# Pairs of heads in one attention stage, results as split columns, a new opening, and a recast difference attention

## The chip, the cores and the metric

The kernel runs on one core of a Trainium2 chip. The metric is the device time of one execution in microseconds (us); the figure for a kernel is the median of several runs. TensorE (PE) does matrix products and transposes (a transpose is a matmul against the identity). VectorE (DVE), ScalarE (ACT) and GpSimd (POOL) do elementwise work, SyncE (SP) issues most DMAs. The engines run their own instruction streams and meet at semaphores. On-chip data lies in SBUF with 128 partitions, products land in PSUM (8 banks).

## The reference

Two transformer blocks run one after the other, both on 256 tokens of width 1024 in float32. What the change touches:

```python
def first_block(x, mem, positions, ...):
    cos_ret, sin_ret = rope_tables(positions, RET_DK)
    cos_mla, sin_mla = rope_tables(positions, MLA_ROPE)
    mem_n = rms_norm(mem, mem_norm)
    for l in range(DEPTH):
        ng = norm_gains[l]
        x = x + 0.5 * rms_norm(swiglu(rms_norm(x, ng[0]), ffn_w_gu[l, 0], ffn_w_down[l, 0]), ng[1])
        h = rms_norm(x, ng[2])
        if l % 2 == 0: tok, qm = retention_mixer(h, ...)
        else:          tok, qm = mla_mixer(h, ...)          # 6 heads, keys 96 wide, values 128
        mem_out = memory_attention(qm, mem_n, mem_w_kv[l])  # 4 heads of 64
        x = x + rms_norm(jnp.concatenate([tok, mem_out], -1) @ w_o[l], ng[3])
        x = x + 0.5 * rms_norm(swiglu(rms_norm(x, ng[4]), ...), ng[5])

def _even_mixer(...):     # second block, layer 0: 256 latent and 256 context tokens
    pl, pc = (jnp.split(a @ w_in, EVEN_SPLITS, -1) for a in (xl, xc))
    hl, hc = _mlstm_bidir(...)                     # 4 heads
    ml = headnorm(h, ml_g) * sigmoid(o)
    lam = exp(sum(lp[0]*lp[1])) - exp(sum(lp[2]*lp[3])) + lam_init
    p = softmax(s)                                  # two maps of scores per head, 4 heads
    da = (p[:, :, 0] - lam * p[:, :, 1]) @ v        # rotated q and k (latent tokens)
    y = jnp.concatenate([ml, headnorm(da, da_g) * (1 - lam_init)], -1) @ w_out
```

The second block's odd layer has a window attention with 16 query heads over 4 key heads; both its layers end with a feed-forward over retrieved experts (PEER).

## The kernel before, in words

**Products.** Every float32 operand is split into a high part (rounded to fp32r) and a low part (the rest), and a product is three matmuls: high by low, low by high, high by high (L251 to L253). Activations lie as columns (feature on the partition) in a "pair" of high and low. Weights come through a ring of three 1 MB slots (tile `ring`, 128x2048), filled by SP in a fixed order (`stream_weights`). ACT makes the high half of a unit of 128x1024 (L223, `split_hi`) and DVE the low half (L230, `split_lo`; POOL does some), into three unit buffers (`units`). In most of the program PE is busy all the time, and DVE and ACT wait for buffers to come free.

**Stages.** `K.block()` is a stage: its engines' code is written out by hand, each engine runs its own list in order, and the end of a stage is a barrier for all of them. The program is a sequence of such stages:

- Opening: SP and ACT issue loads; `norm_to_pair` takes `mem` through root mean square norm, 16 transposes on PE and a split into a pair; `rotary_tables` makes sine and cosine; `spread_conditions` takes the SiLU of the condition vectors; then `norm_to_pair`-like code does the same for x at the entry of the first feed-forward (`feed_forward`, FT = 22 steps; SiLU on ACT, L1337 and two more on DVE per step).
- Layer 0 of the first block: projection (`project`), retention, then memory attention (`attend`), then `columns_to_pair` (PE transposes the mixer's output, ACT and DVE split it) and `quad` work (`multiply_quad`, part of the conditions' product), then the product with w_o.
- Layer 1: the same with latent attention (MLA): `attend` with 12 units, a stage for the memory's transposes, `attend` with 8 units, transposes and split.
- Second block, even layer: the mLSTM attention (`attend_mlstm`), whose stage also holds the projection of the difference attention's rows, and ends with a normalisation of heads on DVE; then `difference_attention`: lambda, rotations of q and k rows, transposes, 16 units of attention, `normalise_heads`, transposes and split into a pair.
- Odd layer: `window_attention`: projections of queries and of keys and values, then a stage for the rotations and for the doubled copies of keys, then transposes and attention.

**A unit of attention** is one head with 128 query rows. PE makes its scores (L1518), DVE their row maxima, ACT the exponentials with their sum, DVE divides, PE transposes the weights (L1526), ACT or DVE copies them out, PE multiplies with the values (L1535). Unit u+1's scores and unit u-1's values stand around the transposes of unit u in PE's list; the buffers are two deep. The difference attention has two maps per unit: DVE takes two maxima (L2050), a scale (L2052), reciprocals (L2063), two factors (L2064, L2065) and the difference (L2068, tile `weights`), and at the end copies the result (L2092, tile `da_out`).

## Time and profile before

| | us |
|---|---|
| median of 3 runs (lowest, highest) | 4476.64 (4474.61, 4479.72) |
| the profiled execution's own time | 4477.14 |
| its span | 4475.3 |
| PE busy | 4097.1 (92%) |
| DVE busy | 2988.9 (67%) |
| ACT busy | 2104.9 (47%) |
| POOL busy | 443.5 (10%) |
| mean granted clock of PE | 0.955 |

The profile is one execution. In a row of stretches "busy" is time in which the engine had an instruction at work, and the clock is the mean share of PE's full speed that was granted: 1.00 is 2.4 GHz and 0.50 is 1.2 GHz. The rest of a span in which PE was not busy is what this change works on; it is spread over the joints between stages.

### The profile page before, as it was taken

How to read it: one execution, taken by the hardware profiler on the slowest of the kernel's cores; microseconds unless marked ns; L12 is line 12 of the kernel's file. 1: busy time of each engine (PE TensorE's matmuls, PEld its weight loads, DVE VectorE, ACT ScalarE, POOL GpSimd, SP SyncE). 2: the span in 40 equal slices, each digit the busy share in tenths (PEclk: the TensorE clock that was granted, in tenths of full speed). 3: DMA queues.
4: the chain of work that ended last, by engine and by line, in shares of the span. 5: the costliest groups of instructions: out<-in, count | busy, mean ns of one | idle time of the engine just before them, and what ended most of it. 6: DMA issues, size and time to landing. Idle time of an engine off the chain costs nothing. (4 is left out here: it accounts for less than half of the span.)

```text
span 4475.3 us, 71173 instructions
## 1 busy us (share of the span) xinstructions
PE 4097.1 (92%) x25224; PEld 3600.8 (80%) x25224; DVE 2988.9 (67%) x5834; ACT 2104.9 (47%) x3223; POOL 443.5 (10%) x488
## 2 busy tenths in 40 slices
PE   6996999968989668999999989999999789999998
PEld 5995889848978558888888888888888578888887
DVE  4555555555546648877777798777776588777776
ACT  4442444434434325555555555555554455555554
POOL 0000000000011105400000162000001045000000
PEclk9997999978989879999999999999999999999999
DMA  5554655554521023255555523555554031555554
GB/s 193 185 197 173 227 199 194 205 202 152 185 109 56 25 89 112 85 188 192 192 187 189 201 86 130 190 188 193 191 211 148 36 138 57 188 190 194 188 189 168
DMA packets 105290, 718.20 MB, mean 160 GB/s; under 512 B 13856, under 2 KB 14464, under 8 KB 21280
## 3 DMA queue, kind: packets, MB, share of 16 engines
q1 hardware_dynamic: 94688, 661.45, 40.5%
q0 software_dynamic: 8880, 52.12, 3.0%
q8 instruction: 107, 1.75, 0.2%
q10 hardware_dynamic: 1552, 2.36, 0.1%
q14 instruction: 63, 0.52, 0.0%
HBM read 709.48 MB, written 6.39 MB: 160 GB/s over the span
## 5 line engine op out<-in xcount | busy, mean ns | idle before, releaser
L230 DVE TENSOR_TENSOR units<-ring,units 128x1024 fp32r<-128x1024 f32 x1128 | 1378.9, 1224 | 562.0 <-ACT units L223 534.3
L223 ACT ACTIVATE units<-ring 128x1024 fp32r<-128x1024 f32 x1206 | 1273.5, 1057 | 1006.7 <-PE ps L253 966.0
L3176 PE MATMUL ps<-wide,units 128*128 128x512 f32 x2904 | 717.5, 389 | 3.3 <-PEq L3062 3.3
L3176 PEld LDWEIGHTS ps<-wide,units 128*128 128x128 f32 x2904 | 544.7, 188 | 117.0 <-issue 3.8
L251 PE MATMUL ps<-units,weighted 128*128 128x512 f32 x1536 | 602.9, 393 | 4.3 <-DVE units L230 4.3
L252 PE MATMUL ps<-units,weighted 128*128 128x512 f32 x1536 | 602.1, 392 | 0.0
L253 PE MATMUL ps<-units,weighted 128*128 128x512 f32 x1536 | 597.5, 389 | 0.0
L3226 ACT ACTIVATE low_halves<-ps 128x256 f32<-128x256 f32 x363 | 139.4, 384 | 623.2 <-PE ps L3178 623.2
L3178 PEld LDWEIGHTS ps<-wide,units 128*128 128x128 f32 x2904 | 396.2, 190 | 28.3
L3178 PE MATMUL ps<-wide,units 128*128 128x256 f32 x2904 | 404.9, 282 | 0.0
L251 PE MATMUL ps<-h_pair,units 128*128 128x256 f32 x1408 | 395.6, 281 | 0.0
L253 PE MATMUL ps<-h_pair,units 128*128 128x256 f32 x1408 | 394.3, 280 | 0.0
L252 PE MATMUL ps<-h_pair,units 128*128 128x256 f32 x1408 | 393.9, 280 | 0.0
L3260 DVE TENSOR_TENSOR gelued<-low_halves,ps 128x256 f32<-128x256 f32 x363 | 153.0, 421 | 315.1 <-ACT low_halves L3226 315.1
L253 PEld LDWEIGHTS ps<-units,weighted 128*128 128x128 f32 x1536 | 288.6, 188 | 62.9
L251 PEld LDWEIGHTS ps<-units,weighted 128*128 128x128 f32 x1536 | 289.9, 189 | 57.3 <-DVE units L230 6.9
L252 PEld LDWEIGHTS ps<-units,weighted 128*128 128x128 f32 x1536 | 289.9, 189 | 46.1
L1337 DVE TENSOR_TENSOR weighted_whole<-gelued,G 128x256 f32<-128x256 f32 x363 | 154.5, 426 | 220.7 <-ACT gelued L3230 215.1
L251 PEld LDWEIGHTS ps<-h_pair,units 128*128 128x128 f32 x1408 | 265.5, 189 | 3.6
L252 PEld LDWEIGHTS ps<-h_pair,units 128*128 128x128 f32 x1408 | 265.0, 188 | 3.8
L253 PEld LDWEIGHTS ps<-h_pair,units 128*128 128x128 f32 x1408 | 265.7, 189 | 0.0
L3095 PE MATMUL ps<-hits 128*128 128x128 f32 x1536 | 231.7, 304 | 9.2 <-POOL hits L3072 9.2
(503 smaller groups left out, 6739.7 us busy)
## 6 DMA issues: line engine op xcount, KB each, us to landing
ring<-in_stream SPq DMA_DIRECT2D x603, 1024.0 KB, 4.8
quad_ring<-in_mod_w POOLq DMA_DIRECT2D x12, 4096.0 KB, 13.9
front<-residuals_dram SPq DMA_DIRECT2D x5, 1024.0 KB, 7.1
gain_rows<-in_norm_gains SPq DMA_DIRECT2D x6, 512.0 KB, 5.0
peer_keys<-in_keys SPq DMA_DIRECT2D x3, 1024.0 KB, 5.1
ml_mask<-in_ml_mask SPq DMA_DIRECT2D x1, 2048.0 KB, 7.7
residuals_dram<-residual SPq DMA_DIRECT2D x2, 1024.0 KB, 7.3
front<-mod_rows_dram SPq DMA_DIRECT2D x4, 512.0 KB, 8.0
```

The costliest lines, as they stand in the source:

```text
L223: act.activation(K.parts(n)[0], K.raw(n), ACT.Copy).then_inc(K.sig("hi_made").sem, 1)
L230: dve.tensor_tensor(lo, K.raw(n), hi.bitcast(FP32), ALU.subtract).then_inc(K.sig("unit_split").sem, 1)
L251: pe.matmul(out, w[0], x[0], start=start, stop=False)
L252: pe.matmul(out, w[0], x[1], start=False, stop=False)
L253: return pe.matmul(out, w[1], x[0], start=False, stop=stop)
L1337: dve.tensor_tensor(whole, a, b, ALU.mult).then_inc(made.sem, 1)
L3095: last = pe.matmul(bank(n)[:, m * KEYS:(m + 1) * KEYS], hits[:, n % BUFFERS, 1, m, :], hits[:, n % BUFFERS, 0, m, :], start=True, stop=True)
L3176: pe.matmul(both, hi[:, k, :], pair[:, :, k, :], start=(k == 0), stop=False)
L3178: last = pe.matmul(both[:, 0, :], lo[:, k, :], pair[:, 0, k, :], start=False, stop=(k == KD - 1))
L3226: act.activation(lows[:, e % 2, :], K.ps[:, 4 + e % 2, SEQ:2 * SEQ], ACT.Copy).then_inc(lows_copied.sem, 1)
L3260: dve.tensor_tensor(gelued[:, e % 2, :], lows[:, e % 2, :], K.ps[:, 4 + e % 2, 0:SEQ], ALU.add)\
```

## The change

**Opening.** x is loaded first, by SP, and then the first three weight slots; `mem`, the positions and the tables' constants come after them. The stages for `mem` and the rotary tables are gone: a class `Opening` puts their work into the feed-forward's steps 18 to 20 (the squares and sines on ACT, angles, tables and the scaling on DVE), and `MemoryHead` puts the 16 transposes and the split of `mem` into chunks 1 and 2 of layer 0's projection. x goes to its pair by the same eight transposed groups as other entries do.

**First block's attentions.** `attend_columns` takes two heads at once (`Two`), three deep: two score products, one DVE maximum over both, two exponentials, a reciprocal and two scalings in place, four transposes, one ACT copy of 128x512, four products with the values as the stationary operand, so that the result comes out as columns; ACT writes its high part and DVE its low part into the pair that the w_o product reads. In layer 0 it holds the memory's 4 paired units; a stage for the 6 remaining columns (with the quad work) follows. In layer 1 one stage holds 6 latent and 4 memory units, and no transposes or split follow.

**Even layer of the second block.** In `attend_mlstm`, ACT takes the squares' sums per unit inside the loop, lambda is computed there, and behind the loop DVE rotates q and k rows, multiplies the gates with the gains and normalises with 16 products. `turned_heads` transposes the mLSTM's columns and q and k in 12 groups of four. The difference attention is again three deep, with one maximum over both maps, a joint factor and one product; its norm (one Square per unit on ACT) ends in the same stage, where each head is transposed and split as soon as it is scaled.

**Window attention.** DVE rotates the query rows under the projection of keys and values (`aside`), and ACT takes half of the key copies.

The diff, cut to its core:

```diff
+class Opening:
...
+    def sync(self, sp):
+        K, ins, loaded = self.K, self.K.ins, self.loaded
+        sp.dma_start(K.x[:, :, :], ins["x"].rearrange("(t p) d -> p t d", p=P)).then_inc(self.x_loaded.sem, 16)
+        stream_weights(K, sp, 0)
+        sp.dma_start(self.pos[:, :], ins["positions"]).then_inc(loaded.sem, 16)
...
+    def scalar(self, act, E):
...
+        act.wait_ge(*self.x_loaded.at(16))
+        for t in range(MT):
+            last = act.activation(E.xs[:, t, :], E.src[:, t, :], ACT.Square, accum_out=E.sums[1][:, t:t + 1])
+        last.then_inc(squared.sem, 1)
+        rstd(K, None, act, E.sums[1], D, squared, mean_done, root_done)
+        split_ahead(K, act, split_hi, K.taken)
...
+    def scalar_step(self, act, f, E):
+        if f == FT - 4:
+            act.wait_ge(*self.loaded.at(96))
+            for t in range(MT):
+                last = act.activation(E.xs[:, t, :], self.mem[:, t, :], ACT.Square, accum_out=self.ss[:, t:t + 1])
...
+    def vector_step(self, dve, f):
...
+        if f == FT - 2:
+            dve.wait_ge(*self.sined.at(1))
+            self.tables(dve)
+            dve.wait_ge(*self.root_done.at(1))
+            self.K.orders["dve"](dve, dve.reciprocal(self.ss, self.ss))
+            for t in range(MT):
+                dve.tensor_scalar(self.mem[:, t, :], self.mem[:, t, :], self.ss[:, t:t + 1], None, ALU.mult)\
...
+class MemoryHead(NormHead):
...
+    def late_tensor(self, pe, c):
+        K = self.K
+        if c == 1:
+            pe.wait_ge(*K.sig("mem_scaled").at(MT))
+        if c in (2, 3):
...
+                    last = pe.transpose(self.bank(k)[:, t * P:(t + 1) * P], self.mem[:, t, k * P:(k + 1) * P], K.ident[:, :])
...
+def attend_columns(K, units, pair):
...
+                for step in range(count + 3):
+                    i = step
+                    if i < count:
+                        if i >= 2:
+                            pe.wait_ge(*weighed.at(i - 1))
+                        for j in range(2):
+                            last = pe.matmul(scores(i)[:, j, :], units[i].q[j], units[i].k[j], start=True, stop=True)
+                        last.then_inc(scored.sem, 1)
+                    i = step - 2
+                    if 0 <= i < count:
+                        pe.wait_ge(*shared.at(i + 1))
+                        if i >= 2:
+                            pe.wait_ge(*copied.at(i - 1))
+                        for j in range(2):
+                            for b in range(MT):
+                                last = pe.transpose(K.ps[:, 4 + i % 2, (j * MT + b) * P:(j * MT + b + 1) * P],
+                                                    exps[:, i % DEEP, j, b * P:(b + 1) * P], K.ident[:, :])
+                        last.then_inc(turned.sem, 1)
+                    i = step - 3
+                    if i >= 0:
+                        pe.wait_ge(*copied.at(i + 1))
+                        if i >= 2:
+                            pe.wait_ge(*taken.at(i - 1))
+                        for j in range(2):
+                            for b in range(MT):
+                                last = pe.matmul(result(i, j), units[i].v[j][b], flipped[:, i % 2, j, b * P:(b + 1) * P],
+                                                 start=(b == 0), stop=(b == MT - 1))
+                        last.then_inc(made.sem, 1)
             @block.vector
             def _(dve):
+                for step in range(count + 4):
...
+                        dve.wait_ge(*scored.at(i + 1))
+                        dve.tensor_reduce(bias[:, i, :], scores(i), AX, ALU.max, negate=True).then_inc(raised.sem, 1)
+                    i = step - 1
+                    if 0 <= i < count:
+                        dve.wait_ge(*weighed.at(i + 1))
+                        order(dve, dve.reciprocal(sums[:, i, :], sums[:, i, :]))
+                        for j in range(2):
+                            row = exps[:, i % DEEP, j, :]
+                            last = dve.tensor_scalar(row, row, sums[:, i, j:j + 1], None, ALU.mult)
+                        last.then_inc(shared.sem, 1)
+                    i = step - 4
+                    if i >= 0:
+                        dve.wait_ge(*rounded.at(i + 1))
+                        dve.tensor_tensor(part(1, i), whole(i), part(0, i).bitcast(FP32), ALU.subtract).then_inc(taken.sem, 1)
...
+                        act.wait_ge(*raised.at(i + 1))
+                        if i >= DEEP:
+                            act.wait_ge(*turned.at(i - DEEP + 1))
+                        for j in range(2):
+                            last = act.activation(exps[:, i % DEEP, j, :], scores(i)[:, j, :], ACT.Exp, bias=bias[:, i, j:j + 1],
+                                                  accum_out=sums[:, i, j:j + 1])
+                        last.then_inc(weighed.sem, 1)
...
+                        act.wait_ge(*made.at(i + 1))
+                        act.activation(part(0, i), whole(i), ACT.Copy).then_inc(rounded.sem, 1)
...
                 dve.wait_ge(*out_taken.at(n_units))
-                for t in range(TILES):
-                    var = K.stat[:, 32 + 7 * t:32 + 7 * t + ML_HEADS]
-                    sq = seen[:, t % 2, :, :].rearrange("p m (h d) -> p (m h) d", d=DV)[:, 0:ML_HEADS, :]
-                    head_stats(K, dve, None, h[:, t, :, :], sq, None, var, ML_HEADS, False)
...
+                dve.wait_ge(*head_squared.at(n_units))
+                dve.tensor_scalar(root, root, 1.0 / DV, EPS, ALU.mult, ALU.add).then_inc(var_done.sem, 1)
+                tmp = seen[:, :, :, :].rearrange("p i m n -> p (i m) n")
+                dve.wait_ge(*rows_taken.at(4))
+                rotate(K, dve, rows[:, MT:TILES, 0:512].rearrange("p t (h d) -> p t h d", d=64), 32, sin, cos, tmp)
+                order(dve, dve.tensor_tensor(gate, gate, row[:, :].unsqueeze(1).broadcast_to([P, TILES, width]), ALU.mult))
+                dve.wait_ge(*rows_taken.at(8))
+                rotate(K, dve, rows[:, MT:TILES, 512:1024].rearrange("p t (h d) -> p t h d", d=64), 32, sin, cos, tmp)
+                dve.wait_ge(*root_done.at(1))
+                order(dve, dve.reciprocal(root, root))
+                    for n in range(ML_HEADS):
+                        d = slice(n * DV, (n + 1) * DV)
+                        last = dve.scalar_tensor_tensor(mix[:, t, d], h[:, t, n, :], root[:, t, n:n + 1], gate[:, t, d],
+                                                        ALU.mult, ALU.mult)
+                order(dve, last)
...
+def turned_heads(K, rows, mix, q, k):
...
+    sources = [[mix[:, t, c * P:(c + 1) * P] for t in range(TILES)] for c in range(4)]
+    for at in (0, 512):
+        sources += [[rows[:, t, at + h * P:at + (h + 1) * P] for t in range(TILES)] for h in range(4)]
...
+                        dve.wait_ge(*scored.at(i + 1))
+                        dve.tensor_reduce(bias[:, i, :], scores(i), AX, ALU.max, negate=True).then_inc(raised.sem, 1)
+                    i = step - 1
+                    if 0 <= i < len(work):
+                        dve.wait_ge(*exped.at(i + 1))
+                        order(dve, dve.reciprocal(share[:, i, :], sums[:, i, 1:2]))
+                        order(dve, dve.scalar_tensor_tensor(share[:, i, :], sums[:, i, 0:1], lam, share[:, i, :], ALU.mult, ALU.mult))
+                        n = keys(i)
+                        dve.scalar_tensor_tensor(exps[:, i % DEEP, 0, 0:n], exps[:, i % DEEP, 1, 0:n], share[:, i, :],
+                                                 exps[:, i % DEEP, 0, 0:n], ALU.mult, ALU.add).then_inc(shared.sem, 1)
...
+                        dve.tensor_scalar(out[:, h, t, :], result(i), sums[:, i, 0:1], None, ALU.mult).then_inc(taken.sem, 1)
...
+                        last = dve.scalar_tensor_tensor(out[:, h, t, :], out[:, h, t, :], square[:, 4 * h + t, :],
+                                                        row[:, h * DV:(h + 1) * DV], ALU.mult, ALU.mult)
+                    last.then_inc(weighed.sem, 1)
...
+                    last = dve.tensor_tensor(pair[:, 1, 4 + h, :], K.ps[:, h, :], pair[:, 0, 4 + h, :].bitcast(FP32), ALU.subtract)
...
-        project(K, pair, KD, TILES, 2 * kv_width, kv)
+        def rotate_queries(dve):
+            rotate(K, dve, qrows[:, :, :].rearrange("p t (h d) -> p t h d", d=WA_DH), 32, sin, cos, tmp)
+        project(K, pair, KD, TILES, 2 * kv_width, kv, aside=rotate_queries)
...
+                        last = act.activation(k2[:, t, :, n, :], heads_of(t), ACT.Copy)
```

The first place is the start of the program on ACT. `x`, `cols`, `ident` are input tiles, `normed` is the normalised x, `h_pair` its pair, `c_silued` the condition. Before:

```order
L1899 ACT_TABLE_LOAD
L1899 ACTIVATE c_silued<-cols 128x16
L1896 UNCONDITIONAL_BRANCH
L1288 UNCONDITIONAL_BRANCH
L353 ACTIVATE normed,stat<-x 128x1024 x2
L302 ACT_TABLE_LOAD
L302 ACTIVATE stat<-stat 128x2
L358 ACTIVATE h_pair<-ps,cols 128x256 x8
L223 ACTIVATE units<-ring 128x1024
```

After:

```order
L1438 DMA ident<-in_ident 128x128
L1439 DMA cols<-in_cols 128x171
L1443 ACT_TABLE_LOAD
L1443 ACTIVATE normed,stat<-x 128x1024 x2
L302 ACT_TABLE_LOAD
L302 ACTIVATE stat<-stat 128x2
L223 ACTIVATE units<-ring 128x1024 x2
L1450 ACTIVATE h_pair<-ps,cols 128x256 x8
L1451 ACT_TABLE_LOAD
L1451 ACTIVATE c_silued<-cols 128x16
L223 ACTIVATE units<-ring 128x1024
```

ACT no longer does a norm of `mem` ahead of that of x (lines 1391 to 1377 above), and x's squares (both halves now) come ahead of its first weight splits (L223).

The second place is PE at the latent attention of layer 1: `mla_q`, `mla_k` queries and keys, `mla_kv` the values, `turned_weights` the transposed softmax weights. Before:

```order
L1518 MATMUL ps<-mla_k,mla_q 128x256 x2
L1526 MATMUL ps<-ident,weights 128x128 x2
L1518 MATMUL ps<-mla_k,mla_q 128x256
L1526 MATMUL ps<-ident,weights 128x128 x2
L1535 MATMUL ps<-mla_kv,turned_weights 128x128 x2
L1518 MATMUL ps<-mla_k,mla_q 128x256
L1526 MATMUL ps<-ident,weights 128x128 x2
L1535 MATMUL ps<-mla_kv,turned_weights 128x128 x2
```

After:

```order
L1689 MATMUL ps<-mla_k,mla_q 128x256 x6
L1698 MATMUL ps<-ident,exps 128x128 x4
L1689 MATMUL ps<-mla_k,mla_q 128x256 x2
L1698 MATMUL ps<-ident,exps 128x128 x4
L1708 MATMUL ps<-turned_weights,mla_kv 128x128 x4
L1689 MATMUL ps<-mla_k,mla_q 128x256 x2
L1698 MATMUL ps<-ident,exps 128x128 x4
L1708 MATMUL ps<-turned_weights,mla_kv 128x128 x4
L1689 MATMUL ps<-mla_k,mla_q 128x256 x2
L1698 MATMUL ps<-ident,exps 128x128 x4
L1708 MATMUL ps<-turned_weights,mla_kv 128x128 x4
L1689 MATMUL ps<-mem_k,mem_q 128x256 x2
```

Two units of one head (two query tiles) are now one pair of heads, six products stand ahead of the first transposes in place of three, and the memory's pairs follow without a gap; the values changed sides in the product.

The third place is DVE in the middle of the difference attention; `small` holds maxima, sums and factors. Before:

```order
L2050 TENSOR_REDUCE small<-ps 128x1 x2
L2052 TENSOR_SCALAR small<-small 128x2
L2092 COPY da_out<-ps 128x128
L2063 RECIPROCAL small<-small 128x2
L2064 TENSOR_SCALAR small<-small,da_lam 128x1
L2065 TENSOR_SCALAR part<-exps,small 128x512
L2068 SCALAR_TENSOR_TENSOR weights<-exps,small,part 128x512
L2050 TENSOR_REDUCE small<-ps 128x1 x2
L2052 TENSOR_SCALAR small<-small 128x2
L2092 COPY da_out<-ps 128x128
```

After:

```order
L2696 SCALAR_TENSOR_TENSOR exps<-exps,small 128x512
L2698 RECIPROCAL small<-small 128x1
L2689 TENSOR_REDUCE small<-ps 128x2
L2693 RECIPROCAL small<-small 128x1
L2694 SCALAR_TENSOR_TENSOR small<-small,da_lam 128x1
L2696 SCALAR_TENSOR_TENSOR exps<-exps,small 128x512
L2698 RECIPROCAL small<-small 128x1
L2703 TENSOR_SCALAR da_out<-ps,small 128x128
L2689 TENSOR_REDUCE small<-ps 128x2
L2693 RECIPROCAL small<-small 128x1
L2694 SCALAR_TENSOR_TENSOR small<-small,da_lam 128x1
L2696 SCALAR_TENSOR_TENSOR exps<-exps,small 128x256
```

A unit now has five DVE instructions ahead of its result's copy in place of seven, and the wide ones are one maximum and one product in place of two maxima, a scaling and a product.

## Rows read from the trace of the kernel before

**Rows 1.** Stretches: length; busy PE, PEld, DVE, ACT, POOL (instructions); clock; DMA share, GB/s.
```profile
0.00:51.03 51.03, 7.52 (x32) 6.54 (x33) 17.31 (x42) 18.66 (x33) 7.64 (x14) 0.83 0.45 170
402.51:436.45 33.94, 29.38 (x144) 20.23 (x145) 12.69 (x39) 11.64 (x31) 1.90 (x3) 0.56 0.03 6
971.77:1024.54 52.77, 41.96 (x208) 31.51 (x209) 27.73 (x94) 25.02 (x75) 1.00 (x2) 0.79 0.20 82
1495.90:1520.26 24.36, 6.07 (x32) 5.90 (x33) 15.69 (x36) 4.47 (x7) 2.70 (x1) 0.65 0.02 6
1503.21:1512.24 9.03, 0.00 (x0) 0.00 (x0) 8.76 (x25) 0.20 (x1) 0.00 (x0) 0.50 0.00 0
1520.26:1590.60 70.34, 44.05 (x208) 29.29 (x208) 43.85 (x128) 25.95 (x80) 0.00 (x0) 0.76 0.00 0
1590.60:1619.48 28.88, 6.02 (x33) 5.84 (x33) 19.76 (x31) 7.88 (x11) 0.00 (x0) 0.60 0.04 10
3476.70:3492.20 15.50, 0.03 (x1) 0.03 (x1) 14.23 (x34) 1.02 (x1) 0.00 (x0) 0.63 0.00 1
3479.23:3486.96 7.73, 0.00 (x0) 0.00 (x0) 7.59 (x12) 0.00 (x0) 0.00 (x0) 0.60 0.01 1
```

**Rows 2.** Timeline of the opening: start, duration, engine, line, operation, tiles, count, idle time.
```profile
9.99 2.36 DVE L230 TENSOR_TENSOR units<-ring,units 128x1024 fp32r<-128x1024 f32 x2 [9.05 <-ACT units L223]
...
24.80 1.42 DVE L1401 TENSOR_SCALAR normed<-mem,stat 128x1024 f32<-128x1024 f32 x2
...
42.51 1.06 ACT L353 ACTIVATE normed<-x 128x1024 f32<-128x1024 f32 x1 [0.86 <-PEq L1896]
...
48.94 3.48 DVE L377 SCALAR_TENSOR_TENSOR h_pair<-ps,cols,h_pair 128x256 fp32r<-128x256 f32 x8 [1.07 <-ACT h_pair L358]
...
51.03 0.56 PE L251 MATMUL ps<-h_pair,units 128*128 128x256 f32 x1
```

**Rows 3.** DMA issues of the first 60 us: size, median time to landing.
```profile
quad_ring<-in_mod_w POOLq DMA_DIRECT2D x1, 4096.0 KB, 17.6
x<-in_x ACTq DMA_DIRECT2D x1, 1024.0 KB, 5.0
...
gain_rows<-in_norm_gains SPq DMA_DIRECT2D x1, 512.0 KB, 8.9
```

**Rows 4.** Timeline, VectorE, end of the first feed-forward.
```profile
232.93 0.42 DVE L1337 TENSOR_TENSOR hid_whole<-silu,ps 128x256 f32<-128x256 f32 x1 [3.27 <-PE ps L253]
```

**Rows 5.** Timeline, TensorE, sixteen transposes at the full clock.
```profile
1346.51 1.95 PE L2182 MATMUL ps<-ident,a 128*128 128x128 f32 x16
```

**Rows 6.** Stretches of memory attention (layer 0, four units) and latent attention (layer 1, nine).
```profile
408.13:418.18 10.05, 10.05 (x33) 6.98 (x32) 4.10 (x16) 3.35 (x13) 0.00 (x0) 0.50 0.00 0
977.60:989.76 12.16, 11.68 (x75) 8.59 (x73) 8.51 (x34) 7.29 (x27) 0.00 (x0) 1.00 0.43 174
```

**Rows 7.** Groups by line and shape, difference attention: busy, mean ns, idle before.
```profile
L2050 DVE TENSOR_REDUCE small<-ps 128x1 f32<-128x512 f32 x16 | 10.3, 682 | 0.0
...
L2050 DVE TENSOR_REDUCE small<-ps 128x1 f32<-128x256 f32 x16 | 6.0, 417 | 2.8 <-PE ps L1518 2.8
...
L2092 DVE COPY da_out<-ps 128x128 f32<-128x128 f32 x16 | 4.6, 285 | 3.8 <-PE ps L1535 3.8
...
L2068 DVE SCALAR_TENSOR_TENSOR weights<-exps,small,part 128x256 f32<-128x256 f32 x8 | 3.9, 485 | 0.3
```

**Rows 8.** Waits in the difference attention: total, times, longest.
```profile
PE ps L1526 <- DVE weights L2068: 25.9, 14, 3.5
```

**Rows 9.** Timeline, ScalarE and GpSimd, end of the mLSTM stage.
```profile
1478.20 1.28 ACT L2482 ACT_TABLE_LOAD   x1
...
1495.69 2.91 POOL L230 TENSOR_TENSOR units<-ring,units 128x1024 fp32r<-128x1024 f32 x1 [7.81 <-ACT units L223]
```

**Rows 10.** Timeline, VectorE, under the projection of the window keys and values.
```profile
3476.49 1.23 DVE L230 TENSOR_TENSOR units<-ring,units 128x1024 fp32r<-128x1024 f32 x1 [8.85 <-ACT units L223]
```

More of the change, by code:

```diff
@@ L1328, in feed_forward @@
     entry_past(K, entry)
+    if opening is not None:
+        opening.past()
     K.taken += FFN_SLOTS
@@ new lines, in _ @@
+                act.wait_ge(*mean_done.at(1))
+                act.activation(square, square, ACT.Sqrt).then_inc(root_done.sem, 1)
+                for h in range(heads):
+                    act.wait_ge(*columns.at(h + 1))
+                    act.activation(pair[:, 0, 4 + h, :], K.ps[:, h, :], ACT.Copy).then_inc(rounded.sem, 1)
+    for signal in (scored, raised, exped, shared, turned, copied, made, taken, squared):
+        signal.past(len(work))
+    row_loaded.past(16), mean_done.past(1), root_done.past(1)
@@ L2581, in window_attention @@
+    for signal in (weighed, columns, rounded):
+        signal.past(heads)
 def window_attention(K, pair, sin, cos, mask, head, spare):
```

893 lines of the change are left out of this document (460 added, 433 removed).

## The prediction

> **What bounds the kernel now.** I read the page first: PE is busy 92% of the span, so away from the joints between stages nothing but fewer or faster matmuls can gain. Then the stretches [rows 1], for the places where PE stands: the opening, 51.03 us with 7.52 of PE (its first product starts at 51.03 [rows 2]); the end of layer 0's mixer (33.94, PE 29.38 at a clock of 0.56); that of layer 1 (52.77, PE 41.96 at 0.79); the way from the mLSTM to the first scores of the difference attention (24.36, PE 6.07); that attention (70.34, PE 44.05 at 0.76, DVE 43.85); its tail (28.88, PE 6.02); and the window's rotations (15.50, PE 0.03). Together 277 us, to which the change is confined. In the waits, the difference attention's transposes stand 25.9 us behind DVE's weights in 14 units [rows 8]. The two clocks are the other half: four memory units took 10.05 us, PE busy throughout at 0.50, while nine latent ones took 12.16 at 1.00 [rows 6], so 2.51 us a unit at 1.2 GHz and 1.35 at 2.4 GHz.
>
> **Part by part**, against the profiled execution's 4477.14, which is 0.5 above the median shown.
>
> *1. Opening.* The chain of x (squares, root, scaling, transposes, split) runs from 42.51 to 51.03, 8.52 us [rows 2]; what stands before it (the norm of `mem`, tables, SiLU) leaves the path. x must now land first. It took 5.0 us when little else was in flight; in the first microseconds the 4 MB of POOL's quad load are (17.6 us), and beside such traffic 512 KB took 8.9 [rows 3]. Bounds 5.8 (issued in the first microsecond, then 5.0) and 14.7 (that, with another 8.9); I take 9.5, near the 8.9. In the chain stand one more table load, 1.28 [rows 9], since the first square no longer finds a loaded table, and two weight splits on DVE ahead of the pair's low halves, 2.36 less the 1.07 that DVE idled there [rows 2], 1.3. First product at 9.5 + 1.28 + 8.52 + 1.3 = 20.6 in place of 51.03: **+30.4** (25 to 34).
>
> *2. What the opening moved.* On DVE one feed-forward step gets the tables, a reciprocal and the scaling: seven small operations at 0.35 (25 of a rotation took 8.76 [rows 1]) and 1.42 for L1401 [rows 2], 3.9 us against 3.27 of idle time before L1337 [rows 4]. ACT gets squares, sines and a root with table switches back to SiLU, in a step where PE's lead of two hidden buffers covers most of it. I charge 1.5 (0 to 5; three switches at 1.28 and the 0.6 that DVE lacks are 4.4). `MemoryHead` adds 16 transposes to PE's list, 1.95 [rows 5]; behind its wait for `mem_scaled` stand the rest of the projection's chunks, but that scaling is a step's work older. SP's list has `mem`, positions and tables behind x and three weight slots, and step 18 needs them 150 us later: nothing. **-3.5** (-8 to -2).
>
> *3. Layer 0.* Eight memory units at 2.51 were 20.1 of the 33.94; the other 13.9 are eight column groups, their split, quad work and joints. Now four pairs: 10.8 at the full clock, 20.1 at half; I take 16 with their filling. Six groups in place of eight leave three quarters of 13.9, 10.4. About 26: **+8** (4 to 12).
>
> *4. Layer 1.* Twelve latent units at 1.35 and eight memory units at 2.51 are 16.2 + 20.1; the rest of 52.77 is a stage of transposes, the mixer's 16 transposes, split and joints, 16.5. Now ten pairs at the full clock are 20 x 1.35 = 27.0, with filling 29; the eight groups' memory transposes and a joint stay, 4.5, and an end of 1.5. 35: **+17.8** (all pairs at half clock 50.2 and 8 of rest, -5, to +20).
>
> *5. mLSTM's end.* The rotations, 8.76 of DVE in 9.03 [rows 1], move before the stage's end. DVE's list from ACT's table load at 1478.20 [rows 9]: rotations 8.8, gates by gains over 128x2048 at twice a split's 1.23 [rows 10], 2.5, sixteen products at 285 (a copy of 128 columns) to 485 ns (a product over 256) [rows 7], 4.6 to 7.8, small ones 0.8. It ends between 1495 and 1499; POOL's split, 1495.69 + 2.91 [rows 9], ends at 1498.6 and covers it, and if DVE were the later only the excess counts. The lambda's DMA was waited for by DVE; now it lands under the loop, its sums hide in DVE's idle time, and the squares are in ACT's. A joint of 0.6 and twelve groups of transposes and copies, 7.8 by the 16 transposes of 1.95 and 128x512 readings of 0.68 [rows 5, 7] on two engines: the first scores at 1507.0 for 1520.26, **+13.3** (10 to 15.5).
>
> *6. The difference attention.* PE's 44.05 at 0.76 is 33.5 at the full clock. DVE's two maxima become one over the same elements, 16.3 in sum [rows 7]; the scaling L2065 goes, as dear as the product L2068 or less (485 ns on 256 columns [rows 7]), some 7 us of 43.85: 37. So at 2.4 GHz the loop is DVE's, 37 and 7 of filling and emptying, if three units in flight cover the waits of rows 8, and 6 for what they don't; at 1.2 GHz it is PE's, 67 and 8. I take 50: **+20.3** (-5 to +24).
>
> *7. Its tail.* 28.88 was a row's DMA, statistics, 16 heads' norms, a stage of transposes and a stage of split. Now the last square 0.45, a table load 1.28 [rows 9], root and reciprocal 0.6, sixteen products at 0.25 to 0.285 [rows 7], 4.0, the last head's transposes and split, four times 0.12 [rows 5] and two readings of 512 columns at 0.68 [rows 7] with handing over, 2.8, a joint 0.6: 9.7, **+19.2** (15 to 21).
>
> *8. Window.* The query rotation, 7.73 [rows 1], goes under the projection, where DVE idled 8.85 before 3476.49 [rows 10]; without that cover it would cost all 7.7 again. ACT takes half of the copies, 0.8. **+8.5** (7 to 9.5).
>
> Sum 30.4 - 3.5 + 8 + 17.8 + 13.3 + 20.3 + 19.2 + 8.5 = 114.0, so 4477.1 - 114.0 = **4363**.
>
> Two rules of the Trainium skill beside the rows. The load of a table takes 1.28 us here [rows 9], and that alone stands in the sum. "ScalarE: Activation LUTs", section "What ACT_TABLE_LOAD costs", adds about 1.38 us of drain to every switch, an estimate of 2.8 us more for the two loads on the path (terms 1 and 7); no row here shows that drain.
>
> **Rivals.**
> - *R1, the clock stays at 1.2 GHz in the merged loops.* For: it was 0.50 in all four memory units, 0.76 on average in the difference attention, and these loops begin after joints where PE stands. Against: the latent units, with the same mixture, ran at 1.00 [rows 6]; the pairs give PE denser work, and it came into layer 1's from a busy stretch. Price: layer 0 at 20 for 16 is 4, layer 1 at 58 for 35 is 23, the difference attention at 75 for 50 is 25, the transposes of term 5 4: 56, so 4419. "TensorE: Matmul & The Clock Gate", "Part 4: PE-mode transpose", in the Trainium skill, says that transposes do not count as PE being busy; half the matmuls of these loops are transposes, and by that rule this rival would hold. The latent units at 1.00, half of whose matmuls are transposes too, disagree.
> - *R2, the opening starves.* x lands late beside the quad, and the first weights, behind it, at 17.6 + 5.0 = 22.6 [rows 3]; with their splits the first product is at 32, not 20.6: 4375. Against: the first low half was begun at 9.99 before, with the quad load in flight [rows 2].
> - *R3, the three units in flight do not overlap.* Then each pair pays its own chain at the full clock, maximum, two exponentials, reciprocal, two scalings, transposes, copy, products, some 5 us (nine to ten steps between 0.3 and 0.7 [rows 7]) for 14 pairs, 70 in place of 45, and each difference unit 6 for 16, 96 in place of 50: 71 more, 4434. For it: the 14 waits of rows 8. Against it: those came with two buffers.
> - *R4, slower than before.* The same chain, with PE's parts at half clock and the handing over between engines no longer hidden: 7 us a pair, 98 for 45, and 8.5 a unit, 136 for 50, 139 in all, with 12 for transposes at half clock, 4514. It decides from where the 30 units cost more than 114 above my terms, some 7 us on average. Against it: the present units take 1.35 to 2.51, and even in the difference attention 70.34/16 = 4.4 [rows 1, 6].
>
> **Chances and range.** Forecast (4340 to 4385) 0.66; R1 0.15; R2 0.10, which lies in that range; R3 0.06; R4 0.03. All terms at their good bounds are 20 more (3.6, 1.5, 4, 2.2, 2.2, 3.7, 1.8, 1), 4343; with 5 for what one execution differs from another, 4338. The high end takes in most of R1, whose loops need not all be slow: 4410. A measurement of this kernel can tell 0.2%, 9 us, from no change. Faster 0.95 (all but R4 and the edge), same 0.02, slower 0.03.
>
> **What would show it.** Right: the first product of the profile near 20 us, x landed near 9.5; PE's steps in feed-forward without a gap of over 2 us around 230; layer 0's attention to first w_o product in 26 and layer 1's in 35; clock 1.00 in most of the merged stages; difference scores start some 7 us behind the stage's end and its loop takes 50; its tail 10; and 7 between the window's projection and its transposes. Wrong: a clock of 0.50 in stage 4 or 6, PE waiting in each pair for DVE's scalings, a first product after 30, or PE gaps in the feed-forward's steps 18 to 21 for ACT's table switches.

## The result, and the profile after

The changed kernel takes 4348.03 us (median of 4 runs, 4345.00 to 4354.13) against 4478.18 for the kernel before (4 runs, 4474.61 to 4484.35): a ratio of 0.971, 95% interval 0.9693 to 0.9726, 130 us faster. In a second comparison (five runs, taken together with the last experiment) it took 4346.34 and the ratio was 0.9706 (0.9693 to 0.9719). The forecast was 4363, 114 us less than the profiled execution before. The profiled execution after took 4354.13, the longest of its four, and its span 4352.3, 123.0 under the span before.

The page after, engines over the span:

```profile
span 4352.3 us, 70792 instructions
PE 4068.3 (93%) x25204; PEld 3579.2 (82%) x25204; DVE 2952.7 (68%) x5733; ACT 2107.7 (48%) x3282; POOL 437.7 (10%) x480
```

The same stretches as in [rows 1], between the same events (columns as there: length; busy PE, PEld, DVE, ACT, POOL; clock; DMA share, GB/s). In order: the opening to the first product, layer 0's first memory scores to w_o, layer 1's transposes to w_o, last projection product to first difference scores, from there to the last result's copy, the tail, and the window's rotations:

```profile
0.00:15.92 15.92, 3.56 (x16) 3.26 (x17) 5.03 (x10) 9.50 (x16) 1.89 (x6) 1.00 0.88 356
373.65:393.48 19.83, 15.56 (x141) 9.81 (x141) 9.28 (x27) 10.14 (x31) 1.59 (x3) 0.80 0.01 3
935.25:964.87 29.62, 25.64 (x193) 20.44 (x193) 20.34 (x58) 21.97 (x69) 1.00 (x2) 1.00 0.37 146
1439.83:1454.19 14.36, 7.68 (x48) 7.50 (x49) 10.43 (x20) 5.41 (x10) 2.31 (x1) 0.76 0.00 0
1454.19:1495.98 41.79, 36.11 (x208) 21.97 (x208) 34.62 (x96) 31.55 (x111) 0.00 (x0) 0.96 0.03 7
1495.98:1505.72 9.74, 4.27 (x16) 2.89 (x17) 7.22 (x23) 4.31 (x8) 0.00 (x0) 0.60 0.00 0
3361.30:3368.21 6.91, 0.00 (x1) 0.03 (x1) 5.80 (x18) 2.36 (x5) 0.00 (x0) 0.77 0.01 1
```

The same matmuls as before in the difference attention (x208) keep PE busy 36.11 us where they took 44.05: not the work got smaller but its clock higher, 0.96 for 0.76. Layer 1 stands at 1.00 for 0.79.

| term | forecast | measured |
|---|---|---|
| 1 opening (51.03 to 15.92) | +30.4 | +35.1 |
| 2 moved into feed-forward and projection | -3.5 | -6.3 |
| 3 layer 0 (33.94 to 19.83) | +8 | +14.1 |
| 4 layer 1 (52.77 to 29.62) | +17.8 | +23.2 |
| 5 mLSTM's end (24.36 to 14.36) | +13.3 | +10.0 |
| 6 difference attention (70.34 to 41.79) | +20.3 | +28.6 |
| 7 its tail (28.88 to 9.74) | +19.2 | +19.1 |
| 8 window (15.50 to 6.91) | +8.5 | +8.6 |
| sum | 114.0 | 132.4 |
| everything else | 0 | -9.4 |

Terms 1, 3, 4 and 6 came out above the ranges that the prediction gave them (up to 34, 12, 20 and 24). The last row is the span's 123.0 less 132.4. It is mostly one execution's own: from layer 0's w_o to layer 1's transposes the profile after has 541.8 us, the one before 535.3, the second profile of the changed kernel 535.2; that second execution's span was 4340.5, 134.8 less than before. Another 3.6 us lie between layer 1's w_o and the mLSTM's last projection product (475.0 for 471.4, and between 471.2 and 475.1 in all other profiles, the kernel before included).

The opening on ACT, start, duration, what it waited for:

```profile
6.11 1.28 ACT L1443 ACT_TABLE_LOAD   x1 [6.11 <-DMA x<-in_x]
7.41 1.06 ACT L1443 ACTIVATE normed<-x 128x1024 f32<-128x1024 f32 x1
...
9.61 1.28 ACT L302 ACT_TABLE_LOAD   x1
10.90 0.20 ACT L302 ACTIVATE stat<-stat 128x2 f32<-128x2 f32 x1
11.28 2.00 ACT L223 ACTIVATE units<-ring 128x1024 fp32r<-128x1024 f32 x2 [0.17 <-DMA ring<-in_stream]
```

x has landed at 6.11, near the good bound of 5.8 and not at 9.5. Behind both table loads the next activation starts 0.01 to 0.02 us later. So the extra drain that the Trainium skill gives for a switch ("ScalarE: Activation LUTs", section "What ACT_TABLE_LOAD costs") is not seen here. From x's landing the chain takes 9.8 us, and the first product starts at 15.92. Less the added table load of 1.28 the chain is 8.53 us, as long as before (8.52): the two weight splits, charged with 1.3, cost nothing.

Why x landed early shows in the DMA queues over the first 6 us (q1 is SP's, q0 is POOL's; packets, MB, share of 16 engines), and then over the next 10:

```profile
q1 hardware_dynamic: 299, 1.27, 55.5%
q0 software_dynamic: 4, 0.03, 1.3%
```

```profile
q0 software_dynamic: 278, 2.28, 54.1%
q1 hardware_dynamic: 272, 1.97, 47.0%
```

POOL issued the quad's 4 MB at 1.29, but they had hardly begun to move when x was there, so x had the DMA engines nearly to itself. The price of the new opening stands later:

```profile
35.50 0.39 PE L251 MATMUL ps<-h_pair,units 128*128 128x256 f32 x1 [2.03 <-DVE units L230]
```

PE, which is 35 us ahead of where it was, stands 2.03 us for weights: ACT's split of them waited for its DMA until 33.13.

DVE's groups by shape in the difference attention, against [rows 7]:

```profile
L2689 DVE TENSOR_REDUCE small<-ps 128x2 f32<-128x1024 f32 x8 | 9.8, 1225 | 3.1 <-PE ps L2655 2.9
L2696 DVE SCALAR_TENSOR_TENSOR exps<-exps,small 128x512 f32<-128x512 f32 x8 | 6.0, 752 | 0.3
L2689 DVE TENSOR_REDUCE small<-ps 128x2 f32<-128x512 f32 x8 | 5.4, 683 | 1.4 <-PE ps L2655 1.4
L2703 DVE TENSOR_SCALAR da_out<-ps,small 128x128 f32<-128x128 f32 x16 | 5.3, 336 | 1.7 <-PE ps L2674 1.7
```

One maximum over 2x512 takes 1225 ns in place of 2 x 682, but two maxima in a row overlap (1.28 us for both in a timeline below), so the joined instruction saves some 0.06 us a unit. And the waits of that attention (engine and line, what they waited for; sum, times, longest), to be read beside [rows 8]:

```profile
PEld ps L2663 <- DVE exps L2696: 9.9, 13, 1.5
ACT exps L2730 <- DVE small L2689: 8.9, 12, 2.3
PE ps L2663 <- DVE exps L2696: 2.2, 5, 1.0
```

The kernel before had these, beside the 25.9 of [rows 8], which is PE's own wait:

```profile
ACT exps L2106 <- DVE small L2052: 39.5, 16, 2.9
PEld ps L1526 <- DVE weights L2068: 38.2, 16, 3.7
DVE small L2063 <- ACT exps L2106: 18.3, 16, 1.5
```

For the softmax weights PE itself now waits 2.2 us in place of 25.9, its weight loads (PEld) 9.9 in place of 38.2, and ACT waits 8.9 for its maxima in place of 39.5.

### The profile page after: what moved, and what is told of

It is laid out like the page before. It is cut to its first block and busy times, and to the rows that moved or that the text cites. A ratio compares the mean times of both kernels' runs of the same rounds, so it can differ in the third digit from the quotient of the medians.

```text
span 4352.3 us, 70792 instructions
## 1 busy us (share of the span) xinstructions
PE 4068.3 (93%) x25204; PEld 3579.2 (82%) x25204; DVE 2952.7 (68%) x5733; ACT 2107.7 (48%) x3282; POOL 437.7 (10%) x480
## 5 line engine op out<-in xcount | busy, mean ns | idle before, releaser
L223 ACT ACTIVATE units<-ring 128x1024 fp32r<-128x1024 f32 x1206 | 1273.0, 1056 | 1005.3 <-PE ps L253 964.8
```

The source lines that it names most:

```text
L223: act.activation(K.parts(n)[0], K.raw(n), ACT.Copy).then_inc(K.sig("hi_made").sem, 1)
```

## The experiments

What is compared is mostly one stretch in one profile. Its scatter can be read from stages that nothing changed in: layer 1's took 29.60 to 29.62 in every kernel that had it, layer 0's 19.8 to 20.5, the way to the difference scores 13.5 to 14.4. The difference attention with its tail, where nothing in it was changed, took 50.5 to 52.1, and shortest where its clock was highest (its loop alone 40.8 at 1.00, 41.8 at 0.96, 42.4 at 0.92). Where nothing else is said, the kernel is the changed one with one edit.

**Two-deep exponentials.**

```diff
-    DEEP = 3
+    DEEP = 2
```

> The exponentials' buffer of both paired attentions is two deep instead of three. If the third buffer is what keeps the loops full, ACT's exponentials of a unit now wait for the transposes of the unit but one before it, and the difference attention's loop (41.8 us in the changed kernel) goes to 50 or more, layer 1's attention (29.6 to the next product) to 34 or more. If the order of the lists and the joined instructions do it (PE is busy 36.1 of the 41.8), both stay within 2 us: the ring of exponentials 1.5, DVE 1.2 and transposes 0.7 has two units to go round in, 1.7 us a unit against the 2.6 that a unit takes.

4344.82 us. Layer 1 took 29.60 and the difference attention with its tail 52.09, against 29.62 and 51.53. The third buffer is worth nothing here; two buffers are enough for the three units that the lists have in flight.

**Two maxima again.**

```diff
-    dve.tensor_reduce(bias[:, i, :], scores(i), AX, ALU.max, negate=True).then_inc(raised.sem, 1)
+    for m in range(2):
+        last = dve.tensor_reduce(bias[:, i, m:m + 1], scores(i)[:, m, :], AX, ALU.max, negate=True)
+    last.then_inc(raised.sem, 1)
```

> In the difference attention DVE again takes a maximum per map, two instructions for one. They cost 0.14 us a unit more (2 x 682 against 1225 ns on 512 keys), 2.2 us in 16 units. If DVE bounds the loop, as the prediction's sixth term has it, 41.8 us becomes 44; if PE does, it stays under 42.8.

4347.63 us. Attention and tail took 53.97, which is 1.9 to 3.4 us above the unchanged ones, and the loop 44.25, as forecast for a loop in which DVE's list counts. But the price was not 0.14 us a unit: the two maxima together take 1.29 us on 512 keys in this profile, and DVE's busy time rose by 0.9 in all (42.73 for 41.84). PE's rose more, 42.97 for 40.38, its clock being 0.83 for 0.89. So this run does not show that DVE bounds the loop; most of its loss may be the clock's.

**The order of the lists.** In both paired attentions the transposes and everything behind them stand one step earlier; maxima, exponentials and scalings stay where they are:

```diff
-    i = step - 2          # PE: transposes; ACT: copies
+    i = step - 1
...
-    i = step - 3          # PE: values
+    i = step - 2
...
-    i = step - 4          # DVE: result
+    i = step - 3
```

> In both paired attentions the transposes of a unit stand one step behind its scores, as in the kernel before, instead of two (and copies, values and results one step earlier too); the joined instructions and buffers stay. If the order of the lists is what hides the chain of maximum, exponentials, reciprocal and scaling, PE now waits for it in every unit: the difference attention from its first scores to w_out (51.5 us) becomes 65 or more with a clock near 0.8, and layer 1's (29.6) 36 or more. If the joined instructions do it, both grow by under 4.

4408.36 us, and this is the largest effect of all. The three stretches of layer 0, layer 1 and the difference attention with its tail:

```profile
372.96:400.32 27.36, 19.30 (x141) 12.49 (x141) 9.75 (x27) 11.03 (x31) 1.59 (x3) 0.60 0.02 4
937.71:983.25 45.54, 29.48 (x193) 23.12 (x193) 20.42 (x58) 23.83 (x69) 1.00 (x2) 0.89 0.24 94
```

```profile
1471.00:1562.63 91.63, 54.33 (x224) 35.34 (x225) 42.60 (x118) 37.28 (x119) 0.00 (x0) 0.66 0.01 3
```

27.4, 45.5 and 91.6 us for 19.8, 29.6 and 51.5. The waits in the difference attention:

```profile
PEld ps L2663 <- DVE exps L2696: 46.0, 15, 4.0
DVE small L2689 <- PE ps L2655: 41.9, 15, 3.8
ACT exps L2730 <- DVE small L2689: 37.7, 15, 3.7
```

All three engines wait for each other once in each unit: PE's next scores stand behind transposes that wait for DVE, and DVE's scaling stands behind the maximum of those scores. The clock falls with it, 0.66 for 0.89, and PE is busy 54.3 for 40.4 on the same matmuls. These three stretches gained 85 us on the kernel before (33.9 + 52.8 + 99.2 against 19.8 + 29.6 + 51.5). With one step less of lag 64 of them are lost.

**The same step alone, in the kernel before.**

```diff
+                  out_ready, out_taken, weights, between=None, lag=1):
...
-        u = step - 1
+        u = step - lag
...
-                              weighed, weighed, turned, copied, out_ready, out_taken, weights)
+                              weighed, weighed, turned, copied, out_ready, out_taken, weights, lag=2)
```

> The kernel before with one thing changed: in its difference attention PE's transposes of a unit stand two steps behind its scores instead of one, the values three, copies and results one step later on ACT and DVE; the instructions, two-deep buffers and stages are its own. If the order of the lists is what the loops gained by, the loop (70.3 us from the first scores to the last result's copy in the profile of before) comes down to what DVE's list takes, 43.9 busy plus filling, 47 to 53, with PE's clock above 0.9. If it takes the joined instructions or the separate score buffers' earlier release as well (before, scores wait until DVE has weighed the unit but one before), it stays above 60.

4477.40 us beside 4475.56: nothing. From the first scores to w_out 98.84 us, 99.22 in the profile before. The loop alone took 69.5, so the second reading came. PE's wait of [rows 8] is gone (1.0 us of 25.9 is left), but PE waits elsewhere, for the copies of the transposed weights, and the two waits of ACT and DVE for each other stand as they were (39.5 and 18.3 before):

```profile
PE ps L1535 <- ACT turned_weights L2116: 10.0, 9, 2.5
ACT exps L2106 <- DVE small L2052: 38.6, 16, 2.9
DVE small L2063 <- ACT exps L2106: 18.5, 16, 1.5
```

A part of DVE's timeline there shows why:

```profile
1545.67 0.28 DVE L2092 COPY da_out<-ps 128x128 f32<-128x128 f32 x1
1547.28 0.17 DVE L2063 RECIPROCAL small<-small 128x2 f32<-128x2 f32 x1 [1.32 <-ACT exps L2106]
...
1548.25 0.75 DVE L2068 SCALAR_TENSOR_TENSOR weights<-exps,small,part 128x512 f32<-128x512 f32 x1
1548.92 1.28 DVE L2050 TENSOR_REDUCE small<-ps 128x1 f32<-128x512 f32 x2
```

DVE weighs a unit before it takes the next maximum, so ACT has no maximum to go on with while DVE waits for ACT: a second ring, of DVE and ACT alone, with nothing to overlap in it, and PE's lag does not touch it. The changed kernel takes the maximum of unit i first and weighs unit i-1 behind it, and hands the score buffer back when the exponentials have read it, not when DVE has weighed. So the lag gains nothing without what else changed: in the difference attention of the kernel before it is worth 0, while the new lists without it are 64 us worse over the three stretches. That the order on DVE is the missing half is read from these waits. Neither that order, nor the earlier release of the scores, nor the joined instructions were put into the kernel before by themselves.

**Layer 1 in two stages.**

```diff
-        attend_columns(K, units + memory_units(mq, mk, mkv), columns)
+        attend_columns(K, units, columns)
+        attend_columns(K, memory_units(mq, mk, mkv), columns)
```

> Layer 1's attention in two stages, six latent pairs and then four memory pairs, instead of one of ten. By the joint alone: one more barrier of about 0.8 us and one more filling and emptying, 4 to 5 us, 29.6 becomes 34, and the memory pairs still run at a clock near 1.00 and about 2.2 us a pair. By the clock: PE stands for some us at the joint, the granted clock falls to 0.5 for the memory pairs as it was for them in the kernel before, they take up to 5 us each, and the stretch becomes 40 or more.

The whole kernel took 4348.09 us and layer 1's stretch 34.03 for 29.62, the joint's 4.4, as by the first reading. The clock did dip, to 0.84 on average over the last 10.55 us of it; it did not stay at the 0.50 that the four units of [rows 6] had.

**x behind the weights.**

```diff
+        stream_weights(K, sp, 0)
         sp.dma_start(K.x[:, :, :], ...).then_inc(self.x_loaded.sem, 16)
-        stream_weights(K, sp, 0)
```

> SP issues the three weight slots first and x behind them. If x's place on the queue is worth what it moves in front of it, x lands 6 to 7 us later (3 MB more at some 430 GB/s), the first product starts near 22 instead of 15.9, and the later wait of PE for weights (2.0 us at 35.5) stays or shrinks. If the engines serve the four loads in parallel and share among them, x lands only 1 or 2 us later and the first product at 17 to 18.

4365.58 us; both readings missed by far. x's row in the list of DMA issues is

```profile
x<-in_x SPq DMA_DIRECT2D x1, 1024.0 KB, 22.1
```

in place of 5.3, and the first product starts at 34.16. The three slots and x on SP's queue are 4 MB and the quad is 4 MB on POOL's; at the 420 or so GB/s of the opening the eight take 20 us. SP's transfers landed one after the other, the slots at 6.1, 11.1 and 16.4, x at 24.3, and from 6 us on POOL's queue took its share. Over 16 to 22 us, when x was under way:

```profile
q0 software_dynamic: 202, 1.65, 66.4%
q1 hardware_dynamic: 206, 0.84, 34.7%
```

The queues moved the same number of packets, but x's are half as large, so x had a third of the rate. That is how x's place came to cost 18 us: a slot behind the first took 5 us beside the quad, not 2.4, and x itself 7.9.

**Everything else out of the opening's way.**

```diff
-        stream_weights(K, sp, 0)
+        stream_weights(K, sp, 9)
         sp.dma_start(self.pos[:, :], ...)
...
+                    pool.wait_ge(K.sig("conditions_spread").sem, 1)
                     load_quad(K, pool, 0)
```

> The quad's 4 MB is issued only when the conditions are spread (near 18 us), and SP issues positions, tables' constants and mem behind nine more weight slots. In the changed kernel x lands 5.3 us after its issue, beside the quad's queue, and PE stands 2.0 us for weights at 35.5. If the two queues share the engines evenly, x alone lands in some 3 us and the first product comes at 13.5 to 14 instead of 15.9, and the wait at 35.5 goes: the start of layer 0's projection 3 to 4 us earlier. If x's landing is set by its own latency and packets, it stays above 5, and only the 2 us of the later wait can come.

4339.10 us. x still takes 5.3 and the first product starts at 15.93: with nothing ahead of it on its queue x is bound by its own way, and the quad had not delayed it. But the wait at 35.5 is gone. From the first product to layer 0's projection it is 199.52 us, and 199.54 in the experiment before this one, where PE comes so late that its weights are there; in the profiles with the loads of the changed kernel it is 201.5 to 203.7, in the kernel before and its two variants 198.5 to 199.9. The tables and squares are in the steps in all of the new ones. So the first half of term 2 is not theirs but late weights: of the 3.9 us between the changed kernel and this one 2.0 is the wait, and 1.9 is PE's busy time (196.16 for 194.28), at a slightly lower clock (0.98 for 0.99).

**The gains as column scales.**

```diff
-                order(dve, dve.tensor_tensor(gate, gate, row[:, :].unsqueeze(1).broadcast_to([P, TILES, width]), ALU.mult))
...
-                    last = dve.tensor_tensor(pair[:, 1, n, :], bank(n), pair[:, 0, n, :].bitcast(FP32), ALU.subtract)
+                    last = dve.scalar_tensor_tensor(pair[:, 1, n, :], bank(n), K.cols[:, C_ML + n:C_ML + n + 1],
+                                                    pair[:, 0, n, :].bitcast(FP32), ALU.mult, ALU.subtract)
```

> The mLSTM's gains are no longer multiplied into the gates on DVE (4.50 us in the changed kernel); they stand as per-partition scales in the copies of the turned columns. The same values come out. If DVE's list sets the end of that stage, the way from the last projection product to the first difference scores, 13.6 to 14.4 us in the four runs so far, gets 2 to 3 us shorter, to where GpSimd's last split ends. If that split or PE's is the later already, nothing changes.

4345.42 us in one run, and the stretch from the last projection product to the first difference scores is 10.30 for 14.36 and 13.48 in the two profiles of the changed kernel:

```profile
1434.40:1444.70 10.30, 5.43 (x49) 5.26 (x49) 5.81 (x11) 5.35 (x10) 2.89 (x1) 1.00 0.00 0
```

In the changed kernel DVE's list did set the end of that stage, not POOL's split: without the product the transposes start 3.3 us behind the last projection product in place of 5.7. Now the split ends last (1434.20 + 3.09, and the transposes start at 1437.73). The rest of the 4.06 is the transposes and what follows, 7.0 us for 8.7, with the clock at 1.00.

**The quad product inside layer 0's attention.**

```diff
+                    if step == 1 and quad is not None:
+                        multiply_quad(K, pe, quad)
```

> Layer 0's quad product (64 matmuls, 3.7 us) moves from the stage of the six columns into the memory attention, behind the first two pairs' scores, where PE otherwise waits for exponentials. Theory of the clock: PE keeps working there, the pairs' remaining matmuls come at a higher granted clock than the 0.73 that they had, and the stretch from the first scores to w_o (19.8 to 20.5 us) falls by 3 or more. Theory of hiding alone: of its 3.7 some 1 us fills PE's wait, the rest is only moved, -1. Against both: the quad's DMA has not landed when PE comes to it, and the attention starts later by that wait; then no gain or a loss up to 3.

4341.65 us in one run; the stretch takes 18.91 for 19.8 to 20.5. Its clock rises, 0.87 for 0.80, and from 379.38 to 386.50, behind the quad's matmuls, it is 1.00 where the same pairs had 0.73. Still only 1 us comes of it, as the theory of hiding alone had it, although the clock did what the other theory says: the quad's matmuls take 5.1 us there, at a mean clock of 0.69 over 374.00 to 379.38, in place of 3.7.

**The window part alone, in the kernel before.** The edit is the window's pieces of the change, and nothing else.

> The kernel before with the window part of the change alone: the query rotation under the projection and half of the key copies on ACT. If the term stands by itself, the stretch from that projection's end to the transposes falls from 15.5 to 7 us and nothing else moves. If the cover depends on the other parts, PE waits for DVE's splits in the projection and some of the 8.6 is lost there.

4468.82 us in one run, and 6.94 us from the projection's end to the transposes for 15.50; the projection of keys and values took 24.75 in both. The term stands by itself. This profile has another thing in it: layer 1's attention, untouched, took 46.07 us in place of 52.77, at a clock of 0.94 for 0.79 (the profile of the lag experiment: 52.43, 0.79). So the 23.2 of term 4 would be 16.5 against this execution.

**The changed kernel and the three gains together.** Its edits are those of the loads, the gains and the quad.

> The changed kernel again, beside the next one on the same chip: 4344 to 4354, a ratio of 0.970 to 0.972 to the kernel before.

> The loads moved back, the gains in the columns and the quad in layer 0's attention together. If the three act on different waits and all are on the path, their stages keep what they showed alone: 2 to 4 us before layer 0's projection, 3.3 before the difference scores, 1 in layer 0's attention and up to 1 behind it, 7 to 9 in all, a ratio of 0.968 to 0.970. If what one saves is waited for later (the weights' stream, which runs ahead by three slots only), less than 4.

The changed kernel 4346.34 (4342.34 to 4350.59), ratio 0.9706 (0.9693 to 0.9719); with the three edits 4340.40 (4338.17 to 4341.86), ratio 0.9688 (0.9675 to 0.9702), to the same nine runs of before (4479.99). The ranges of the five runs each don't meet, the difference is 5.9 us. The parts: first product to projection 199.18 for 203.36, to the difference scores 11.40 for 13.48, layer 0 19.26 for 20.06, 7.1 in sum. That is the low end of the forecast 7 to 9, and the 5.9 of the medians are below it: the difference scores gained 2.1 and not the 3.3 that they did alone, at a clock of 0.85 where it was 1.00, and the attention behind them took 52.08 for 50.53. It has the lowest median of the versions that were run more than once. The one run of the loads alone, 4339.10, lies inside its range, so what the other two edits add to them is not shown by the whole kernel's time.

## Why the prediction was right, and where it was not

- **Sum and sign.** 4363 forecast, 4348 measured, inside the range. The places were right, and the two gains whose mechanism was a plain removal, terms 7 and 8, came within 0.1. That the total lies so near is in part luck: the terms together were 18.4 us too small, four of the eight beyond their own ranges, and 9.4 us of the profiled execution that belong to no term took half of it back.
- **Term 1, under-sized by 4.7.** x landed at 6.11, not 9.5, which is 3.4: taking the row of 512 KB beside other traffic as the nearest was the error, for the quad's load had moved 0.03 MB when x was there. The other 1.3 were charged for two weight splits that cost nothing. R2 did not come. Its argument against itself was misread: the low half begun at 9.99 before had no quad load in flight, which POOL issued only at 40.69 there. Its danger is real but lies elsewhere, in what is put on SP's queue ahead of x (first product 34.16), and in 2 us given back at 35.5.
- **Term 2, 6.3 for 3.5.** The transposes are there (2.8 with clock; 2.0 in the second profile, for 1.95). The other 3.5, for a charge of 1.5, do not come from the work in the feed-forward's steps but from the weight stream, as the late loads show.
- **Terms 3, 4 and 6, under-sized by 20.** Three units in flight do cover the waits, but it is the places in the lists that put them in flight; the third buffer, which the prediction set against R3, is worth nothing. All three were priced from the unit times of the kernel before. In term 4 ten pairs with filling were to take 29 us and took 23.9 (939.70 to 963.61), less than twenty of the old units at full clock (27.0). In term 6 I had DVE busy 37 and 13 beside it for filling and waits; it was busy 34.6 and 7.2 us came on top. In term 3 the four pairs took 11.55 for 16, though at a mean clock of 0.65, and the rest of the stretch 8.28 for 10.4.
- **Term 5, over-sized by 3.3.** Gates by gains took 4.50 for 2.5, the sixteen products 6.38 for 4.6 and one rotation step 2.1 more than its like; DVE ended last, not the split. That moved the transposes back by 2.4. The other 0.9 are the transposes and what follows, 8.7 for 7.8, at a clock of 0.73. The reason for DVE's times stands under the hardware below.
- **R1** did not come: 1.00 and 0.96. The prediction set the rule of the Trainium skill on transposes ("TensorE: Matmul & The Clock Gate", "Part 4: PE-mode transpose") beside it, with half the matmuls of these loops transposes. They are 4 of a pair's 10 instructions and, as a product leaves two matmuls in the trace, a quarter of the matmuls: 40 of 160 in layer 1's loop, 48 of 208 in the difference attention, 18 of 73 in the latent units of [rows 6]. Three quarters are products, so neither those units nor these loops settle whether the rule holds. Only layer 0, which starts after 11 us of idle PE, had 0.80.
- **R3** and **R4** did not come, but the order experiment is R3's mechanism, and at its 27.4 + 45.5 + 91.6 the clock had fallen as in R4. It costs 64 us, 4408 in all, somewhat less than the 4434 I gave R3. So most of the gain in these loops depended on one offset in each list.

## What to carry to other kernels

Where engines hand units round in a ring, look first at where each engine's list places the next unit's first step against the last unit's closing step, on every engine of the ring; here PE's list in the old order lost 64 of 85 us, and PE's list alone in the new order gained nothing, as did a third buffer. Where PE no longer waited, its granted clock was higher too (0.76 to 0.96 in the difference attention), so the gain was larger than PE's waits of 25.9. When a program starts 35 us earlier, its loads are the next bound: here it paid to put the first consumer's tile first on its queue (18 us) and everything that is needed later behind more of the stream (4 us).

## What the hardware showed unexpectedly

GpSimd's and VectorE's elementwise work block each other for whole instructions. Three times while GpSimd split a unit, a DVE instruction that reads two tiles of SBUF took some 2.1 us longer than its shape does. DVE's timeline in the changed kernel:

```profile
1427.09 4.50 DVE L2444 TENSOR_TENSOR ml_vo<-ml_vo,row 128x2048 f32<-128x2048 f32 x1
1431.62 2.53 DVE L1582 TENSOR_TENSOR seen<-da_rows,axial 128x256 f32<-128x256 f32 x1
...
1435.98 0.42 DVE L1582 TENSOR_TENSOR seen<-da_rows,axial 128x256 f32<-128x256 f32 x1
...
1438.54 6.38 DVE L2452 SCALAR_TENSOR_TENSOR even_mix<-ml_h,stat,ml_vo 128x128 f32<-128x128 f32 x16
```

and GpSimd's:

```profile
1427.02 2.42 POOL L230 TENSOR_TENSOR units<-ring,units 128x1024 fp32r<-128x1024 f32 x1 [10.25 <-ACT units L223]
1430.41 3.46 POOL L230 TENSOR_TENSOR units<-ring,units 128x1024 fp32r<-128x1024 f32 x1 [0.98 <-ACT units L223]
1439.63 2.51 POOL L230 TENSOR_TENSOR units<-ring,units 128x1024 fp32r<-128x1024 f32 x1 [5.76 <-ACT units L223]
```

The same L1582 takes 0.42 without and 2.53 with; twice a split's 1.23 is 2.46, an estimate for L2444, which took 4.50; the sixteen products took 6.38 here and, in the kernel with the gains in the columns, 4.29, where the third split began only in their last microsecond. "SBUF — State Buffer" in the Trainium skill, section "Terms", says that the port pair of the two engines is locked for a full instruction and that the loser blocks; these rows agree, 2.04 to 2.11 us a time. GpSimd loses too: its second split, begun while L2444 ran, took 3.46 us for 2.42. Three splits cost term 5's list 6.2 us.
